# The last pairs of a state-space core: outputs issued one pair later, the first norm and the first output slab moved into the core

## The reference, cut to what matters

```
def ssd_mixer(h, ...):                       # 32 heads of 64 channels in 8 groups
    ...                                      # projection, convolution, silu, softplus of dt
    y = y_fwd + y_bwd + xs * d_skip          # decay matrix times C.B per head, times x
    y = y.reshape(b, s, D_INNER) * silu(z)
    y = rms_norm_2(y.reshape(b, s, g, 256), norm_g.reshape(g, 256))   # one norm per group
    return y.reshape(b, s, D_INNER) @ w_out  # 2048 -> 1024
```

## Time and profile before

| what | value |
|---|---|
| times of the three runs | 1721.7, 1724.6, 1727.01 us |
| their median | 1724.6 us |
| span of the profiled execution | 1723.2 us |
| TensorE busy | 1700.8 us, 99% of the span |
| VectorE busy | 1385.6 us, 80% |
| ScalarE busy | 993.5 us, 58% |
| mean granted TensorE clock | 0.998 of full speed |

### The profile page before, as it was taken

One profiled execution on the slowest core, in us unless ns is written; L12 is line 12 of the kernel. 1 busy time (PEld: TensorE's weight loads), 2 busy tenths in 40 slices (PEclk: granted clock), 3 DMA queues, 4 the chain that ended last, 5 costly groups with the idle time before them and its releaser, 6 DMA issues.

```text
span 1723.2 us, 29149 instructions
## 1 busy us (share of the span) xinstructions
PE 1700.8 (99%) x11414; PEld 1540.2 (89%) x11414; DVE 1385.6 (80%) x2193; ACT 993.5 (58%) x1578; POOL 26.5 (2%) x37
## 2 busy tenths in 40 slices
PE   8999999999999999999999899999999999999999
PEld 8799998999998988889998698888888888798888
DVE  5778888888888888899986879888988876866654
ACT  6565545766554555446677756553655456865542
POOL 0300000000000000000000100000000000000000
PEclk9999999999999999999999999999999999999999
DMA  9245468444547777795442057779677845035552
GB/s 373 98 171 196 172 219 317 181 162 172 195 171 277 278 286 280 277 358 185 180 174 98 25 196 262 273 282 345 259 277 280 313 168 189 25 147 195 193 178 93
DMA packets 62436, 367.06 MB, mean 213 GB/s; under 512 B 6944, under 2 KB 7328, under 8 KB 27776
## 3 DMA queue, kind: packets, MB, share of 16 engines
q1 hardware_dynamic: 61776, 362.70, 57.2%
q0 software_dynamic: 560, 3.01, 0.4%
HBM read 364.64 MB, written 1.05 MB: 212 GB/s over the span
## 4 chain that ended last, share of the span: by engine, by line
PE 88%; DVE 6%; ACT 3%; DMA 2%; issue 1%; SPq 0%; DVEq 0%; ACTq 0%
PE psum L504 17%; PE psum L525 11%; PE psum L379 11%; PE psum L381 11%; PE psum L380 11%; PE psum L506 9%; PE psum L527 6%; PE psum L432 4%; DVE lo L1868 1%; PE psum L494 1%; DMA raw<-slabs_dram 1%; PE psum L572 1%; ACT hi L1234 1%; DMA modw<-wmod_dram 1%; PE psum L497 1%
## 5 line engine op out<-in xcount | busy, mean ns | idle before, releaser
L1868 DVE TENSOR_TENSOR lo<-raw,hi 128x1024 fp32r<-128x1024 f32 x522 | 619.5, 1225 | 162.2 <-ACT hi L1234 162.1
L1234 ACT ACTIVATE hi<-raw 128x1024 fp32r<-128x1024 f32 x522 | 522.8, 1051 | 344.9 <-PE psum L527 191.5
L504 PE MATMUL psum<-XHL,hi 128*128 128x512 f32 x1280 | 452.5, 399 | 0.0
L379 PE MATMUL psum<-XHL,hi 128*128 128x256 f32 x1320 | 375.9, 285 | 1.5 <-DVE lo L1868 1.5
L380 PE MATMUL psum<-XHL,hi 128*128 128x256 f32 x1320 | 373.5, 283 | 0.0
L381 PE MATMUL psum<-XHL,lo 128*128 128x256 f32 x1320 | 373.4, 283 | 0.0
L506 PE MATMUL psum<-XHL,lo 128*128 128x256 f32 x1280 | 359.5, 281 | 0.0
L525 PE MATMUL psum<-HHL,hi 128*128 (+1 forms) x960 | 338.8, 398 | 0.4 <-DVE S L2058 0.4
L504 PEld LDWEIGHTS psum<-XHL,hi 128*128 128x128 f32 x1280 | 240.5, 188 | 59.7
L527 PE MATMUL psum<-HHL,lo 128*128 (+1 forms) x960 | 269.5, 281 | 0.0
L379 PEld LDWEIGHTS psum<-XHL,hi 128*128 128x128 f32 x1320 | 253.2, 192 | 4.3 <-issue 2.4
(11 more groups left out here) (342 smaller groups left out, 2027.6 us busy)
## 6 DMA issues: line engine op xcount, KB each, us to landing
raw<-slabs_dram SPq DMA_DIRECT2D x269, 1024.0 KB, 5.3
modw<-wmod_dram SPq DMA_DIRECT2D x144, 512.0 KB, 5.4
raw<-slabs_dram SPq DMA_DIRECT2D x4, 512.0 KB, 7.5
A<-small_dram POOLq DMA_DIRECT2D x1, 1536.0 KB, 13.7
X<-x_dram SPq DMA_DIRECT2D x4, 256.0 KB, 4.7
out_dram<-X SPq DMA_DIRECT2D x3, 256.0 KB, 2.3
cond<-cvec_dram POOLq DMA_DIRECT2D x1, 512.0 KB, 8.0
A<-tab_dram POOLq DMA_DIRECT2D x1, 512.0 KB, 15.6
```

The source lines that it names most:

```text
L379: mm(dst, wh, xh, start=start, stop=False, skip_group_check=True)
L504: mm(dst, hi[:, k, j * P:(j + 1) * P], XHL[:, kt, :, :].rearrange("p a t -> p (a t)"), start=start, stop=False, skip_group_check=True)
L1234: f(hi[:, k % SPLIT, at], raw[:, n % RAW, at], ACT.Copy).then_inc(q["hi_ready"], 1)
L1868: v.tensor_tensor(lo[:, k % SPLIT, at], raw[:, n % RAW, at], hi[:, k % SPLIT, at].bitcast(F32), ALU.subtract).then_inc(q["lo_ready"], 1)
```

## The change

On TensorE the outputs of pair p are issued in iteration p+1, behind both exponent steps of that iteration, with the sums of group (p-4)/2 ahead of them at even pairs from 4 on, and `spread(0)` ahead of the outputs of pair 11. Behind the loop come the first four column tiles of output slab 0 (24 matmuls, banks 4 and 5), the outputs of pair 15, the other four column tiles (banks 6 and 7), then `spread(1)`. The stage's four zeroing matmuls are left out, and the sums of group 6 move into `ssd_rest(1)`. The group sums go to spare columns of bank 2 or 3. On ScalarE the squares of group g follow `exps(4g+7)`, and `round_y(0)` follows `exps(28)`. On VectorE `diagonal(0)` and `diagonal(1)` move from head 28 to head 20, `scale_group(0)` from head 30 into `gate_y(11)`, `group_rest(0)` from behind the last product to head 29. No load and no wait of the SP queue changes.

```diff
--- before.py
+++ after.py
@@ -320,6 +320,15 @@
 
             return evacuated[s % 2], (EV0, OD0)[s % 2][name] + s // 2 + 1
 
+
+        def group_bank(g):
+
+            at = T + 2 * (g == SSD_G - 1)
+            return bank[2 if g < SSD_G - 2 else 3][:, at:at + 2]
+
+        def spread_bank(g):
+
+            return bank[g % 4][:, 0:T] if g else bank[3][:, T:2 * T]
 
         def ssd_count(s):
 
@@ -615,10 +624,10 @@
                                      xh, xl, start=False)
                 return last.then_inc(q["slab_used"], 1)
 
-            def down_stage(stage, before=None):
+            def down_stage(stage, before=None, begun=0):
 
                 pe.wait_ge(q["h_ready"], HID[stage] + 1)
-                for b in range(4, 8):
+                for b in range(8 if begun else 4, 8):
                     mm(bank[b][:, 0:2], zero[:, :], zero[:, 0:2], start=True, stop=False,
                        skip_group_check=True)
                 loops = SLABS[stage] // 4 if SLABS[stage] > 8 else 0
@@ -626,7 +635,7 @@
                     with pe.Fori(0, loops) as i:
                         for s in range(4):
                             down_slab(stage, s, i)
-                for s in range(4 * loops, SLABS[stage] - 1):
+                for s in range(4 * loops + begun, SLABS[stage] - 1):
                     if before is not None:
                         before(s)
                     down_slab(stage, s)
@@ -931,9 +940,10 @@
             def group_sums(g):
 
                 pe.wait_ge(q["ysq_folded"], g + 1)
+                to = group_bank(g)
                 for j in range(2):
                     at = g % 2 * 512 + j * P
-                    last = mm(bank[3][:, T + j:T + j + 1], S[:, at:at + P], ones[:, 0:1],
+                    last = mm(to[:, j:j + 1], S[:, at:at + P], ones[:, 0:1],
                               start=(j == 0), stop=(j == 1), skip_group_check=True)
                 last.then_inc(q["ysum_ready"], 1)
 
@@ -943,7 +953,25 @@
                 if g >= 4:
 
                     pe.wait_ge(q["yn_ready"], g - 3)
-                mm(bank[g % 4][:, 0:T], ones, A2[:, g, :], start=True, stop=True).then_inc(q["yspread_ready"], 1)
+                mm(spread_bank(g), ones, A2[:, g, :], start=True, stop=True).then_inc(q["yspread_ready"], 1)
+
+            def outputs(pair):
+
+                if pair < 2:
+                    pe.wait_ge(*ssd_count((24, 21)[pair]))
+                else:
+                    pe.wait_ge(q["yz_ready"], pair - 1)
+                if pair % 2 == 0 and pair >= 4:
+                    group_sums((pair - 4) // 2)
+                if pair == 11:
+                    spread(0)
+                pe.wait_ge(q["mt_ready"], 2 * pair + 2)
+                for j in range(2):
+                    for row in (0, 64):
+                        last = mm(bank[2 + pair % 2][row:row + 64, 0:T], XST[:, pair, j, row:row + 64],
+                                  MT[2 * pair % 4 + row // 64][:, j * T:(j + 1) * T], start=(j == 0), stop=(j == 1),
+                                  skip_group_check=True)
+                last.then_inc(q["y_ready"], 1)
 
             for pair in range(16):
                 if pair < 15:
@@ -952,41 +980,41 @@
                     pe.wait_ge(*ssd_count(23))
                 if pair % 2 == 0 and pair < 14:
                     cb(pair // 2 + 1)
-                if pair % 2 and 3 <= pair < 15:
-                    group_sums((pair - 3) // 2)
                 if pair < 15:
                     expo(2 * pair + 3)
-                if pair < 2:
-                    pe.wait_ge(*ssd_count((24, 21)[pair]))
-                if pair >= 2:
-
-                    pe.wait_ge(q["yz_ready"], pair - 1)
-                if pair == 15:
-                    spread(0)
-                    group_sums(6)
-                pe.wait_ge(q["mt_ready"], 2 * pair + 2)
-                for j in range(2):
-                    for row in (0, 64):
-                        last = mm(bank[2 + pair % 2][row:row + 64, 0:T], XST[:, pair, j, row:row + 64],
-                                  MT[2 * pair % 4 + row // 64][:, j * T:(j + 1) * T], start=(j == 0), stop=(j == 1),
-                                  skip_group_check=True)
-                last.then_inc(q["y_ready"], 1)
-
-            spread(1)
+                if pair:
+                    outputs(pair - 1)
 
             def ssd_rest(s):
                 if s == 1:
                     pe.wait_ge(q["yz_ready"], 16)
                     for g in range(2, 6):
                         spread(g)
+                    group_sums(SSD_G - 2)
                     group_sums(SSD_G - 1)
                 if s == 3:
                     spread(6)
                 if s == 4:
                     spread(7)
 
+            def first_output(ms):
+
+                n = N0["ssd_out"]
+                for m in ms:
+                    for kk in range(2):
+                        last = three(bank[4 + m // 2][:, m % 2 * T:(m % 2 + 1) * T], n, kk * KD + m,
+                                     HH[:, kk, :], HL[:, kk, :], start=(m % 2 == 0 and kk == 0))
+                return last
+
+            pe.wait_ge(q["decay_made"], SSD_H - 1)
+            pe.wait_ge(q["h_ready"], HID["ssd_out"] + 1)
+            pe.wait_ge(q["lo_ready"], 2 * SPLITS[N0["ssd_out"]] + 2)
+            first_output(range(0, 4))
+            outputs(15)
             pe.wait_ge(q["decay_made"], SSD_H)
-            down_stage("ssd_out", ssd_rest)
+            first_output(range(4, KD)).then_inc(q["slab_used"], 1)
+            spread(1)
+            down_stage("ssd_out", ssd_rest, begun=1)
 
             gated_stage("g01_up", 8)
             gated_stage("g10_up", 9)
@@ -1700,16 +1728,17 @@
                 f(S[:, g % 2 * 512:(g % 2 + 1) * 512].rearrange("p (a t) -> p a t", a=2),
                   A1[:, 2 * g:2 * g + 2, :], ACT.Square).then_inc(q["ysq_ready"], 1)
 
-            for h in range(2, SSD_H):
-                exps(h)
-                if h % 4 == 2 and h >= 6:
-                    group_squares((h - 6) // 4)
-
             def round_y(g):
                 act.wait_ge(q["yn_ready"], g + 1)
                 f(HH[:, 2 * g:2 * g + 2, :], A1[:, 2 * g:2 * g + 2, :], ACT.Copy).then_inc(q["yh_ready"], 1)
 
-            round_y(0)
+            for h in range(2, SSD_H):
+                exps(h)
+                if h % 4 == 3 and h >= 7:
+                    group_squares((h - 7) // 4)
+                if h == 28:
+                    round_y(0)
+
             split_hi(N0["ssd_out"] + 1)
             round_y(1)
             group_squares(SSD_G - 1)
@@ -2447,12 +2476,15 @@
 
                 t = S[:, 2048 + pair % 2 * T:2048 + (pair % 2 + 1) * T]
                 dve.wait_ge(q["y_ready"], pair + 1)
-                if pair % 2 and pair >= 3:
-
-                    dve.wait_ge(q["ysum_ready"], (pair - 1) // 2)
-                    kept = v.tensor_copy(tiny[:, 61 + pair:63 + pair], bank[3][:, T:T + 2])
-                    if pair in (5, 13):
+                if pair % 2 == 0 and pair >= 4:
+
+                    g = (pair - 4) // 2
+                    dve.wait_ge(q["ysum_ready"], g + 1)
+                    kept = v.tensor_copy(tiny[:, 64 + 2 * g:66 + 2 * g], group_bank(g))
+                    if g in (1, 5):
                         kept.then_inc(q["ysum_kept"], 1)
+                if pair == 11:
+                    scale_group(0)
                 step.link(stt(out=t, in0=XS[:, pair, :], scalar=col("skip", pair),
                               in1=bank[2 + pair % 2][:, 0:T], op0=ALU.mult, op1=ALU.add))
                 v.tensor_tensor(A1[:, pair, :], A1[:, pair, :], t, ALU.mult).then_inc(q["yz_ready"], 1)
@@ -2466,7 +2498,7 @@
             def scale_group(g):
                 dve.wait_ge(q["yspread_ready"], g + 1)
                 for k in (2 * g, 2 * g + 1):
-                    last = stt(out=A1[:, k, :], in0=A1[:, k, :], scalar=col("snorm", k), in1=bank[g % 4][:, 0:T],
+                    last = stt(out=A1[:, k, :], in0=A1[:, k, :], scalar=col("snorm", k), in1=spread_bank(g),
                                op0=ALU.mult, op1=ALU.mult)
                 last.then_inc(q["yn_ready"], 1)
 
@@ -2494,14 +2526,13 @@
                     dve.wait_ge(*ssd_count(24))
                     step.link(stt(out=A1[:, 14:16, :], in0=two(LAST_TANH), scalar=1.0, in1=A1[:, 14:16, :],
                                   op0=ALU.add, op1=ALU.mult))
-                if h == 28:
+                if h == 20:
                     dve.wait_ge(q["yroot_ready"], 1)
                     diagonal(0)
                     diagonal(1)
-                if h == 30:
-                    scale_group(0)
-
-            group_rest(0)
+                if h == 29:
+                    group_rest(0)
+
             gate_y(14)
             gate_y(15)
             scale_group(1)
@@ -2514,7 +2545,7 @@
             diagonal(5)
             scale_group(2)
             dve.wait_ge(q["ysum_ready"], 8)
```

(2 more changed lines are left out.)

## The result

Five runs of the changed kernel took 1727.5, 1730.5, 1732.1, 1732.5 and 1734.3 us, median 1732.13, against 1724.6 before. The ratio is 1.0037 (95% interval 1.0026 to 1.0048), so the change made the kernel slower by 0.37%, about 6.4 us. I had forecast 1726.3 us, between 1721.0 and 1729.8. The profiled execution was the fastest of the five, with a span of 1725.7 us, 2.5 us above the one before. So its profile shows less than the five runs cost, and the granted clock of each run says why: its mean was 0.998 in the profiled run and 0.993 to 0.995 in the four others. Two things differ even between the two profiled executions: this one has no fall of the clock in the latent stage, where the one before has one of 6.8 us, and it has one behind output slab 0.

The account below looks back on a forecast made before the run. The prediction took the core to be bound by a ring of waits among ScalarE, VectorE and TensorE, no engine being full. Span 1723.2 - 0.8 + 2.5 (clock) = 1724.9, plus 1.4 gives 1726.3 us, range 1721.0 to 1729.8.

Parts of the forecast that it names:

- The gain of the core: Core: shorter period of a group, about 6.2 us instead of 6.97, moving VectorE's last product 3.6 us earlier.
- both gaps: Tail, behind output slab 0: TensorE idle about 1.5 us before spread(2) and 3.4 us before spread(4).
- the clock's term: Behind the tail's idle stretches: TensorE falls to half clock once, costing 2.5 us, bounds 1.6 to 3.4.
- the rest: Core and tail without the clock's fall: output slab 1 starts 0.8 us earlier net.
- VectorE's share of a group: Core: VectorE's own work per group, 6.09 us of the 6.97 us period, taken as its lower bound.
- my own sign of being wrong: Tail: prediction is wrong if the clock's fall lasts much longer than the latent stage's at 1435.
- waits of 1.3 us cost no clock: Core's tail: TensorE's waits of 1.3 us for products left the clock up; an argument for the clock staying up.
- The 1.4 us added to the span: Whole kernel: 1.4 us added to profiled figures, from span 1723.2 to the runs' median 1724.6 us.
- the first case: The forecast itself: gap opens in the tail and the clock falls, 1726.3 us, own range 1724.3 to 1728.5, chance 0.60.
- The gap not opening: Tail: VectorE's work is covered and slab 1 starts 5.8 us earlier, 1718.8 us; chance 0.08.
- The clock staying up: Tail: the gap opens but TensorE's clock does not fall, 1723.8 us; chance 0.20.
- The slower case: Core: the period stays, its 5.6 us of waits are not saved, slab 1 is 3.4 us later, 1731.4 us; chance 0.07.

Follow-up runs that it names:

- The fastest kernel with folds: Against the changed kernel, spread(1) right behind the last outputs, diagonals of groups 4 and 5 ahead of the low halves of slab 1: 1719.5, then 1721.0 us.

## Why the prediction was wrong

**What held.** The mechanism did. The gain of the core is not passed on: the outputs of pair 15 come earlier, slab 1 doesn't. The place and length of both gaps were forecast: 1.5 and 3.4 us, measured 1.45 and 3.01. So was the distance from the last outputs to `scale_group(1)`: forecast 4.6, measured 984.08 - 979.47 = 4.61, and the hold-up of the outputs by the half slab: forecast 0.8, measured 979.47 - 977.76 - 0.74 = 0.97. The clock's fall behind the gap came, and filling the gap took 3.6 us off. What failed are sizes: the clock's term was 2.5 us, and the reruns put it at 3.5 and 4.6; the rest was -0.8 us, and they put it at 0.5 and -0.2.

**First wrong term: the core.** I moved the last product by -3.6 us; it moved by -1.9. The term left out, put at nothing without a reason, is what a fold on GpSimd does to a VectorE sum beside it. VectorE's share of a group was read from rows in which no sum ran beside a fold: there the fold started at 948.02, when VectorE was in a product and then idle. In the new order six folds of the core fall on a sum of two SBUF operands: six rows of 0.84, 0.78, 0.59, 0.78, 0.77 and 0.77 us where 0.42 was, 2.0 us in all, against 1.7 that were missing. The waits in VectorE's list, which I had 4.1 us lower (5.6 - 0.5 - 1.0), came out 4.5 lower from the first product to the last, which makes up the difference.

That the stretch comes from the folds was shown by the kernel without them. Each of the six sums ended 1.00 to 1.02 us after its fold began, though they started anywhere from 0.16 to 0.42 us behind it: by these rows a sum is not slowed, it stands still until about 0.6 us of the fold are over. The low halves fit: started 0.04 us behind a fold, they took 0.55 us longer. I had a row that could have told me: `split_lo` of slab 1 took 2.90 us and other slabs 2.35. The Trainium skill has the rule ("GPSIMD Engine Reference", Specifications): GpSimd's SBUF interfaces are shared with VectorE, and instructions with two SBUF inputs are in contention. The trace agrees: 0.78 in place of 0.42 us for such a sum and 0.69 in either case for the product that takes one operand from PSUM.

Removing the folds would not have won the 1.7 us. The fastest kernel with folds (second profile) and without them had no fall of the clock in the core, and the last product stands 52.9 us after the first C.B product in both: without stretches VectorE waits 1.9 us more for outputs, which TensorE makes later because its sums are longer.

**Second wrong term: the price of one fall.** I took 2.5 us from bounds of 1.6 and 3.4. In the profiled execution the two spreads and two sums took 993.04 - 989.61 = 3.43 us in place of 1.6, and 14 matmuls of slab 1 came 0.21 us apart in place of 0.12, 1.3 us: 3.1 us together. The groups by clock say 3.3 us for a step from 1.000 to 0.998. In the two other profiles the fall lasted 10.2 us and not the 6.7 of rows 8, and by the same count it cost about 4.4 and 4.0 us. That it might last much longer than the one at 1435 was my own sign of being wrong. In the first profile slab 1 was 2.9 us late and not 0.8 early, 3.7 us from the forecast: 1.9 from the core and 1.8 from the clock.

**Third, and the one that broke the range: how many falls.** I charged one fall in one place. By the mean clocks the changed kernel has it in every run, and 18 of 28 runs stood at 0.995 or lower, which takes at least one more. The profiles show two places for it. One is the latent stage, where the kernel before has its own: six of the twelve profiles with the new core order have a fall there, and six don't. The other is the core, where seven of the twelve show one between 970 and 982. In two of these seven all of slab 0 stands behind the outputs, and the fall follows the wait of 2.3 us for the last product. In the five others it comes at a stretch in which TensorE waits about 1.0 us for ScalarE twice within 2 us, here in the changed kernel's first profile, where the clock stayed at 1.00:

```profile
971.11 0.44 PE L900 MATMUL psum<-acr,selr 128*128 128x384 f32 x1 [1.01 <-ACT EX L1667]
...
972.88 0.44 PE L900 MATMUL psum<-acr,selr 128*128 128x384 f32 x1 [0.92 <-ACT EX L1667]
```

I had read 'waits of 1.3 us cost no clock' from one execution. What I called noise of the measurement, 0.3%, is in this kernel mostly this clock: before, too, its runs range from 1720.4 to 1727.2 us as their mean clock goes from 1.000 to 0.997. One of the first five runs stood at 0.998 and four lower, and their median, 1732.1, lies above my range. The later medians of the same kernel, 1728.2 and 1729.3, lie inside it. So by how much the first figure missed is in part the draw of five runs; that the change loses more than I said, 3.6 to 6.4 us and not 1.7, is not.

**Small slips in the working.** The 1.4 us added to the span compare one execution with the median of others; every run on record took 1.7 to 1.9 us more than its own span. And from its own terms the first case reaches from 1724.4 to 1728.2, not 1724.3 to 1728.5. Neither matters beside the three terms above.

**The rivals.** The gap not opening had 0.08 and was rightly low. The clock staying up had 0.20, and no run of 28 shows it. The slower case had the right sign for another reason: the period did not stay at 6.97, it is 6.3.

**Open.** I found nothing in a profile ahead of a fall that says which execution gets one inside the core or in the latent stage. Nor is it shown why the first five runs cost 6.4 us more where the same kernel cost about 3.6 and 4.5 in the later jobs. A fall inside the core in the old order of TensorE was seen once, in the kernel with only the squares moved; the one profile of the kernel before has none, which is too few to say how often it comes.

## What to carry to other kernels

When work is moved ahead of a wait on a saturated engine, ask which producer's list was covered by that work where it stood: here slab 0 had hidden some 5 us of VectorE's tail, and half of it in front of `spread(1)` took the cover away. Start the chain first (one spread of 0.45 us), and put what releases others ahead of what only prepares one's own next step (two diagonals ahead of two low halves): these two moves turned 4 us lost into 4 to 6 us won. Read several executions' mean clocks before calling a spread of times noise: here the gap with an idle stretch of 3.0 us cost some 3.6 us more in half clock.

## What the runs showed of the hardware

TensorE's clock fell from 2.4 to 1.2 GHz after 5 us in which it had two spreads to do and nothing else (984.1 to 989.4), and stayed there for 6.8 us, in two other executions for 10.2, though matmuls were dense again from 993.0; filled with matmuls, the same stretch kept 1.00. It also fell inside the core, at about 971.8 in the last profile of the changed kernel, behind waits of 1.01 and 0.92 us, where TensorE was busy for 2.99 of 4.00 us (966 to 970) and then 1.08 of 2.00; that I had not expected. The Trainium skill ("TensorE: Matmul & The Clock Gate", Why this matters for your kernels) warns of idle gaps between bursts; in this kernel the clock fell also where no gap was over 1.2 us. A fold of 0.73 us on GpSimd held up a VectorE sum that started 0.24 us behind it by 0.36 us.
